# Running the sample's selection and small attention between the tiles of group B's heads, with two heads' columns per projection tile

## The reference

```python
h = _rmsnorm(x, pre_w)
z = h @ w_in                                   # (1024 + 8 rows) x 2048 @ 2048 x 6980
qa, ka, va, ga, qs, ks, vs, gs, qi, ki, wi = _split_cols(z)
...
oa = _diff_attention(qa[..., 0, :], qa[..., 1, :], k_split[..., 0, :], k_split[..., 1, :], va_all, lam, q_pos, k_pos)
oa = _rmsnorm(oa, sub_w) * (1.0 - lam_init)
oa = oa.reshape(b, t, D_A) * jax.nn.silu(ga)   # group A, 8 heads
ob = _dsa_attention(qs, ks_all, vs_all, qi, ki_all, wi, q_pos, k_pos, topk)
ob = ob.reshape(b, t, D_B) * jax.nn.silu(gs)   # group B, 8 query heads on 2 key-value heads
o = jnp.concatenate([oa, ob], axis=-1) @ w_out
x = x + _rmsnorm(o, post_w)
x = x + jax.nn.sigmoid(x @ w_pg + b_pg) * (p @ w_pe)

# inside _dsa_attention, per block of queries
rel = jax.nn.relu(jnp.einsum('bqhd,bsd->bqhs', qqi, ki))
score = jnp.where(vis, jnp.einsum('bqhs,bqh->bqs', rel, ww), -jnp.inf)
_, idx = lax.top_k(score, topk)                # 256 positions per query
kg, vg = k[idx], v[idx]
s = jnp.where(ok, jnp.einsum('bqngd,bqknd->bqngk', qq, kg) * scale, -jnp.inf)
o = jnp.einsum('bqngk,bqknd->bqngd', jax.nn.softmax(s, axis=-1), vg)
```

## Time and profile before

| what | value |
|---|---|
| median of 3 runs | 3878.92 us (3878.88 to 3885.64) |
| profiled execution, its time | 3885.66 us |
| its span in the trace | 3884.0 us, mean granted clock 0.945 |
| PE busy | 3462.2 us, 89% of the span |
| PEld busy | 2731.1 us, 70% |
| DVE busy | 1499.6 us, 39% |
| ACT busy | 845.5 us, 22% |
| POOL busy | 511.6 us, 13% |

### The profile page before, as it was taken

One profiled execution on the slowest core, in us unless ns is written; L12 is line 12 of the kernel. 1 busy time (PEld: TensorE's weight loads), 2 busy tenths in 40 slices (PEclk: granted clock), 3 DMA queues, 4 the chain that ended last, 5 costly groups with the idle time before them and its releaser, 6 DMA issues. The chain is left out here.

```text
span 3884.0 us, 51115 instructions
## 1 busy us (share of the span) xinstructions
PE 3462.2 (89%) x19443; PEld 2731.1 (70%) x19473; DVE 1499.6 (39%) x2854; ACT 845.5 (22%) x1870; POOL 511.6 (13%) x464
## 2 busy tenths in 40 slices
PE   5979999999998988997186899899889999999999
PEld 3667677777776666775133777777768888788887
DVE  2037777777767777622562111111100002311111
ACT  4011344444421212121001122222210002200000
POOL 0002333333332323300003000000000000000000
PEclk9989999999999999998597899999999999999999
DMA  9775677776776756743002011110310111210102
GB/s 343 247 216 147 225 238 255 230 256 222 255 232 216 223 202 219 243 143 104 0 1 65 22 28 39 42 29 6 130 53 24 43 38 62 92 49 24 49 24 87
DMA packets 357958, 497.61 MB, mean 128 GB/s; under 512 B 59793, under 2 KB 280234, under 8 KB 356578
## 3 DMA queue, kind: packets, MB, share of 16 engines
q1 hardware_dynamic: 353440, 486.12, 39.1%
q0 software_dynamic: 1536, 4.20, 0.4%
q10 hardware_dynamic: 2770, 4.46, 0.3%
HBM read 466.81 MB, written 27.90 MB: 127 GB/s over the span
## 5 line engine op out<-in xcount | busy, mean ns | idle before, releaser
L1155 PE MATMUL Z<-W,hT 128*128 128x256 f32 x4608 | 1073.7, 389 | 3.0 <-PEq L116 3.0
L1155 PEld LDWEIGHTS Z<-W,hT 128*128 128x128 f32 x4608 | 869.3, 193 | 210.5 <-issue 97.7
L2079 PE MATMUL Z<-W,hT 128*128 128x256 f32 x2048 | 455.7, 381 | 4.3 <-PE DB L2090 2.3
L2012 PE MATMUL Z<-W,hT 128*128 128x256 f32 x2048 | 446.5, 380 | 1.3 <-ACT small L2141 1.3
L2079 PEld LDWEIGHTS Z<-W,hT 128*128 128x128 f32 x2048 | 390.2, 191 | 61.0 <-issue 7.8
L2012 PEld LDWEIGHTS Z<-W,hT 128*128 128x128 f32 x2048 | 389.2, 191 | 57.2 <-issue 4.6
L781 POOL TENSOR_TENSOR big<-big,qib 128x256 f32<-128x256 f32 x256 | 232.8, 927 | 874.6 <-DMA big<-in_cache_idx_k_dram 718.6
L928 DVE TENSOR_REDUCE page_sc<-big 128x16 f32<-128x1024 f32 x256 | 309.5, 1209 | 1.2 <-POOL big L785 0.6
L917 DVE TENSOR_TENSOR big<-big,qb 128x1024 f32<-128x1024 f32 x192 | 258.5, 1347 | 63.7 <-DMA qb<-zs_d 45.9
L1715 PE MATMUL Z<-W,hT 128*128 128x256 f32 x896 | 210.1, 395 | 0.0
L1715 PE MATMUL DB<-W,hT 128*128 128x256 f32 x896 | 198.8, 380 | 0.0
(11 more groups left out here) (483 smaller groups left out, 3457.0 us busy)
## 6 DMA issues: line engine op xcount, KB each, us to landing
big<-in_cache_diff_k_dram SPq DMA_DIRECT2D x256, 512.0 KB, 4.5
big<-in_cache_diff_v_dram SPq DMA_DIRECT2D x256, 512.0 KB, 5.0
W<-in_w_in_dram SPq DMA_DIRECT2D x27, 2048.0 KB, 10.0
W<-in_w_in_dram SPq DMA_DIRECT2D x72, 512.0 KB, 7.1
W<-in_w_in_dram SPq DMA_DIRECT2D x16, 1024.0 KB, 7.2
W<-in_w_out_dram SPq DMA_DIRECT2D x8, 2048.0 KB, 12.3
W<-in_w_ple_gate_dram SPq DMA_DIRECT2D x8, 2048.0 KB, 8.2
big<-in_cache_idx_k_dram SPq DMA_DIRECT2D x256, 32.0 KB, 4.1
```

The lines of the kernel that those rows point to most:

```text
L1155: mm = pe.matmul(Z[b][:, 0:CW], hT[:, 8 * f + k, n * P:(n + 1) * P], Wr[:, q % 3, k, :], start=(f == 0 and k == 0), stop=(f == 1 and k == 7))
L2012: mm = pe.matmul(Z[t % 2][:, 0:CW], hT[:, k, t * P:(t + 1) * P], W[:, s, k, :], start=(k == 0), stop=(k == KT - 1))
L2079: pe.matmul(Z[b][:, 0:CW], hT[:, k, t * P:(t + 1) * P], W[:, 1 - s, k, :], start=(k == 0), stop=(k == KT - 1))
```

## The change

The tail of group A, the selection and group B's heads become one block. The queries and gates of group B are projected in eight chunks of 256 columns that each hold one kind, queries or gates, of a pair of heads. Their weights come as contiguous 256 columns in halves of 1 MB (`half`, a ring of three), and a tile is projected in two half tiles of 8 matrix products (`project(c, n, f)`). Chunk 0, the first pair's queries, is projected first, with the threshold's counts 0 to 15 between its 16 half tiles. Then 64 tile slots follow, four pairs `s` of 16 slots `x`; slot `k = 16 s + x` is tile `t = k % 8` of head `h = k // 8`. Chunks 1 to 7 are projected in the first 56.

On TensorE a slot is: scores of tile `k`, place 0, first half tile, place 1, transposes of the probabilities, in some slots the output's transposes (`turn`) or new queries (`queries`), place 2, second half tile, place 3, value product. At a place a step of the selection may stand (`decode`). Scores now use `S[0]` alone, the transposes `S[1]`; a projection accumulates in `Z[0]` or `Z[1]`, the value product goes to `TB`, and all decode steps use `DB`. Counts 16 to 32 stand in slots 0 to 8, ranks in 9 and 10, the one-hots of the eight rows in slots 12 to 19 (picks to slot 20), keys and row scores in 23 to 30, the softmax from 31, values in 35 to 42, and the sample's final normalization from 43. The one-hot ring has eight rows, and the picks go to four column groups of the array (`32 * g`), which the copy `picked` takes out. The gathers stand in GpSimd's sequence behind two heads' gate products, four buffers of key or value rows in a ring.

Also: the gate products go from VectorE to GpSimd (`silu`, `output`), except for the last head's; VectorE scales the value product without the gate (`natural`). A pair's rotation is done at once, in slot `x = 8`. Stores of group B's transposed outputs go to SyncE's queue. The last two heads' transposed outputs are copied straight into `hT`, with no store and no read back. The sigmoids stand in slots `x = 0` and `x = 2` of a pair, the last two in slots 56 and 57.

What leaves TensorE's sequence in the selection and in the heads:

```diff
-for n in range(33):
-    pe.wait_ge(b_cnt, n + 1)
-    pe.matmul(TB[:, 0:NB], ones[:, :], cnt, start=True, stop=True).then_inc(b_tot, 1)
...
-for n in range(NPG):
-    u = b * NPG + n
-    pe.wait_ge(b_oh, u + 1)
-    mm = pe.matmul(dst[0:2, 0:TOPK], ids[:, u, :], oneh[:, u % 4, :], start=(n == 0), stop=(n == NPG - 1))
-    mm.then_inc(b_ohu, 1)
-    if n % 2 == 0:
-        k = n // 2
...
-for t in range(NT):
-    pe.wait_ge(h_x, NT * H + t + 1)
-    for f in range(F(t + 1) - F(t)):
-        pe.wait_ge(h_tf, 1 + FB * H + F(t) + f)
-        turned(lambda b: e12[:, t % 2, b * P:(b + 1) * P], f, min(4, t + 1 - 4 * f))
-        if f == 0 and t + 1 < NT:
-            scores(m, u, t + 1)
-    if not last:
-        project(m1, u1, t)
-    pe.wait_ge(h_tf, 1 + FB * H + F(t + 1))
-    pe.wait_ge(h_o, 1 + NT * H + t)
-    for b in range(t + 1):
...
```

TensorE now, chunk 0 and the slots:

```diff
+NPAIR = HB // 2
+NSLOT = 2 * NT
+QCHUNK = {0: 0, 1: 1, 3: 2, 5: 3}
+GCHUNK = {2: 0, 4: 1, 6: 2, 7: 3}
+chunk_at = lambda s, x: 1 + 2 * s + x // NT if s < NPAIR - 1 else (7 if x < NT else None)
+RANK_AT, HOT_AT, K_AT, SOFT_AT, V_AT, END_AT = 9, 12, 23, 31, 35, 43
...
+for i in range(4 * NT // 2):
+    n = 2 * (i // 4) + i % 2
+    project(0, n, i % 4 // 2)
+    total(i)
...
+queries(0)
+queries(1)
+for s in range(NPAIR):
+    for x in range(NSLOT):
+        k, t, h = NSLOT * s + x, x % NT, 2 * s + x // NT
+        c = chunk_at(s, x)
+        scores(k)
+        decode(k, 0)
+        if c is not None:
+            project(c, t, 0)
+        decode(k, 1)
+        pe.wait_ge(h_x, k + 1)
+        if k:
+            pe.wait_ge(h_tc, k)
+        else:
+            pe.wait_ge(h_qc, 2)
+        for b in range(t + 1):
+            mm = pe.transpose(S[1][:, b * P:(b + 1) * P], e12[:, k % 2, b * P:(b + 1) * P], ident[:, :])
+        mm.then_inc(h_t, 1)
+        if s and x in (3, 5):
+            turn(2 * s - 2 + (x == 5))
+        if s < NPAIR - 1 and x in (10, 15):
+            queries(2 * (s + 1) + (x == 15))
+        if s == NPAIR - 1 and x == 11:
+            turn(HB - 2)
+        decode(k, 2)
+        if c is not None:
+            project(c, t, 1)
+        decode(k, 3)
+        pe.wait_ge(h_tc, k + 1)
+        if k:
+            pe.wait_ge(h_nat, k)
+        else:
+            pe.wait_ge(h_qc, 2)
+        for b in range(t + 1):
+            mm = pe.matmul(TB[:, 0:HD], pT[:, b, :], vg[:, h // 4, b, :], start=(b == 0), stop=(b == t))
```

TensorE, the decode steps at the places:

```diff
+def decode(k, place):
+    if k < RANK_AT and place in (1, 3):
+        n = 16 + 2 * k + place // 2
+        if n < 33:
+            total(n)
+    r = k - RANK_AT
+    if r in (0, 1) and place in (1, 3):
+        pe.wait_ge(b_eq, 1 + r)
+        if place == 3:
+            pe.wait_ge(b_prc, r + 1)
+        pe.matmul(DB[:, 0:NB * NS], ones[:, :] if place == 1 else below, eqm, start=True, stop=True).then_inc(b_pre, 1)
+    b = k - HOT_AT
+    if 0 <= b <= NB:
+        if place == 0 and b >= 1:
+            pick(b - 1, 24)
+        if place == 1 and b >= 1:
+            pick_turn(b - 1)
+        if place >= 1 and b < NB:
+            pick(b, 8 * (place - 1))
+    b = k - K_AT
+    if 0 <= b < NB:
+        if place == 1:
+            key_turn(b)
+        if place == 3:
...
```

VectorE, the decode steps of a slot (behind its maximum), the order in a slot, and the one-hots:

```diff
+if k < RANK_AT:
+    bit(15 + 2 * k)
+    if 16 + 2 * k < 32:
+        bit(16 + 2 * k)
...
+if HOT_AT <= k < HOT_AT + NB:
+    for lo in range(0, NPG, 8):
+        one_hot(k - HOT_AT, lo, lo + 8)
...
+for s in range(NPAIR):
+    for x in range(NSLOT):
+        k = NSLOT * s + x
+        if k:
+            natural(k - 1)
+        maximum(k)
+        decode(k)
+        if s < NPAIR - 1 and x == NT:
+            rotate(s + 1)
+        if s == NPAIR - 1 and x == NSLOT - 1:
...
```

```diff
+def one_hot(b, lo, hi):
+    rk3 = three(rkm)
+    for n in range(lo, hi):
+        u = b * NPG + n
+        if u >= 8:
+            dve.wait_ge(b_ohu, u - 7)
+        dve.tensor_scalar(oneh_at(u), iotaj, rk3[:, b, n:n + 1], None, ALU.is_equal).then_inc(b_oh, 1)
```

ScalarE in a slot:

```diff
...
+exps(k)
+if HOT_AT + 1 <= k < HOT_AT + 1 + NB:
+    picked(k - HOT_AT - 1)
+act.wait_ge(h_t, k + 1)
+if k:
+    act.wait_ge(h_pv, k)
+act.activation(pTf[:, 0:(t + 1) * P], S[1][:, 0:(t + 1) * P], ACT.Copy).then_inc(h_tc, 1)
+if s and x in (3, 5):
+    turned(2 * s - 2 + (x == 5))
+if s < NPAIR - 1 and x in (10, 15):
+    queries(2 * (s + 1) + (x == 15))
+if s == NPAIR - 1 and x == 11:
+    turned(HB - 2)
+if K_AT <= k < K_AT + NB:
+    act.wait_ge(b_kt, k - K_AT + 1)
+    act.activation(ktb, DB[:, :], ACT.Copy).then_inc(b_ktc, 1)
+if k == SOFT_AT + 1:
+    act.wait_ge(b_sc, NB + 2)
+    act.activation(ssb[:, 0:257], ssb[:, 0:257], ACT.Exp, scale=SC_B, bias=rmax, accum_out=rsm).then_inc(b_e, 1)
+if k == END_AT + 1:
+    act.wait_ge(b_o, 2)
+    act.activation(sqa, DB[:, 192:256], ACT.Sqrt, scale=1.0 / HD, bias=eps).then_inc(b_qs, 1)
```

GpSimd's gate products and gathers, and SyncE's loads of half chunks:

```diff
+for s in range(NPAIR):
+    if s:
+        for h in (2 * s - 2, 2 * s - 1):
+            silu(h)
+            output(h)
+    if s == 1:
+        pool.wait_ge(b_idx, 1)
+        pool.wait_ge(h_st, 16)
+        for j in range(NB + 4):
+            gather(j)
+    if s == 2:
+        for j in range(NB + 4, 2 * NB):
+            gather(j)
```

```diff
+def half(q):
+    c = q // 2
+    if q >= 3:
+        sp.wait_ge(h_wu, q - 2)
+    lo = QS + 2 * HD * QCHUNK[c] if c in QCHUNK else GS + 2 * HD * GCHUNK[c]
+    sp.dma_start(Wr[:, q % 3, :, :], win[:, 8 * (q % 2):8 * (q % 2) + 8, lo:lo + CW]).then_inc(h_w[q % 3], 16)
```

## The result

The changed kernel takes 3622.18 us (median of 4 runs, 3618.84 to 3625.59), the kernel before 3881.77 us beside it (4 runs, 3878.88 to 3885.64): a ratio of 0.9331, with a 95% interval of 0.9315 to 0.9347.

A forecast was written before the change was run, and what follows sets the result against it. TensorE bounds the heads, while some 330 us of single-step chains hold little matrix work. Terms of 782 us replace 1032, giving 3629 us against the median; 3632 us was said, range 3595 to 3705.

The forecast's parts named there:

- tail of A: From group A's last value product into the new block: only a wait for stores and a barrier left, 5 us.
- chunk 0 with counts 0 to 15: First pair's query projection with threshold counts between half tiles: 3.8 us per step, 65 us in all, bounds 60 and 72.
- change to the slots: Between chunk 0 and the first slot: rotation, two sets of transposes and two copies, uncovered, 7 us, bounds 5 and 10.
- seven heads and decode work: Slots with projections: 571 us for heads at 80.7 each plus slot changes, and 57 us for the selection and attention steps.
- last head: Final slots, without projection and with one score buffer: steps follow one another, 62 us, bounds 42 and 85.
- end: Behind the heads, up to the output projection: last store and reload gone, normalization and last transposes remain, 15 us.
- the cover that the prediction named: In chunk 0, VectorE's 2.6 us per count run under the next half tile, with 0.9 us to spare.
- The held slots: Rival, slots with projections: late VectorE makes TensorE wait at the transposes, heads stay near 90 us, 3695 us; chance 0.14.
- the picks' term: Slots with one-hots: TensorE waits partly for one-hots and the picks cost 2 us, 3.8 per row, 31 in all.
- the rival of the low clock: Last head: serial steps drop TensorE to 1.2 GHz, doubling some 22 us of work, 3654 us; inside the forecast's 0.68.
- The search was not hidden: Rival, counts and picks: all their VectorE time falls on TensorE's path, 112 us more, 3745 us; chance 0.06.
- The slower case: Rival, all slots: waits keep TensorE's clock at 0.50, tiles take 14.2 us instead of 7.1, about 4030 us; chance 0.03.

The follow-up runs named there:

- The run without the cover: Against the changed kernel, every slot's first half tile stands behind the transposes of the probabilities instead of ahead of them; 3786.8 us, ratio 0.9756.
- the filling products: Changed kernel plus unused matrix products in the last head's slots, four ahead of the transposes and two ahead of the value product; 3611.3 us, ratio 0.9296.

## Why the prediction was right, step by step

| term | predicted, us | measured, us | read from |
|---|---|---|---|
| tail of A | 5 | 5.2 | stretch |
| chunk 0 with counts 0 to 15 | 65 | 62.2 | stretch |
| change to the slots | 7 | 7.5 | stretch |
| seven heads and decode work | 571 + 57 | 624.8 | ends of value products |
| last head | 62 | 63.5 | stretch |
| end | 15 | 14.8 | 2568.6 to 2583.4 |
| sum | 782 | 778.0 | |

The sum is 4 us high. Another 3 of the 10 us stand between the 3629 that the sum gives and the 3632 that was said, for which no reason was given. The last 3 are the run: the stages that did not change were 13 us shorter in the trace after, of which 10 drop out against the medians (the profile before lay 6.7 us above its median, the one after 3.3 below).

Where the 253.9 us went, by the same rows: the selection and the small attention had taken 328, and chunk 0 and the decode work take 62.2 and 60.6, which is 205 less; the heads take 564 without the decode work instead of 633, 69 less; tail and end give 9. The last head gives back 21.5, the change to the slots 7.5. What else changed (gate products on GpSimd, stores on SyncE's queue, the last outputs straight into `hT`) was not tried one by one.

**Tail and chunk 0.** Right. One step of chunk 0, as the timeline has it:

```profile
1823.63 0.28 PE L1860 MATMUL DB<-big,ones 128*128 128x8 f32 x2
1823.77 3.70 PE L1801 MATMUL Z<-W,hT 128*128 128x256 f32 x16
1827.30 0.28 PE L1860 MATMUL DB<-big,ones 128*128 128x8 f32 x2
```

The pitch is 3.67 us, where 3.8 were taken (the term is 3 us high), and no row shows idle time: the cover that the prediction named is there. The second half of the weights came in time.

**Seven heads.** The 80.7 us of matrix work per head were measured as 80.7 in head 6, and as 80.0 to 82.0 without the decode work; the 0.1 per slot for one more change of operand did not show. The run without the cover shows that heads and decode work both hang on the half tile ahead of the transposes. The held slots did not come: 1.0 us of waits for exponentials in 56 slots.

**Decode work.** Nearly right in size (57; 60.6), but not in its parts. Counts and ranks were put at 7 and cost 2: 0.8 us is what head 0 lost with its counts, and 1.3 what head 1 has over head 6 with the ranks alone. The picks were put at 31 and cost 35.9. The step said that TensorE would stand idle for the one-hots; the trace has only 1.9 us of idle time there, and the wait shows as long pick rows: eight picks take 0.39 us where their rows are ready and 2.11 where each one waits for VectorE. In slot 16 and slot 17 of the changed kernel:

```profile
2062.16 0.39 PE L1867 MATMUL DB<-page_sc,big 128*2 128x256 bf16 x8
...
2062.88 2.11 PE L1867 MATMUL DB<-page_sc,big 128*2 128x256 bf16 x8
...
2071.51 2.35 POOL L1455 TENSOR_TENSOR seen<-seen,scr 128x1024 f32<-128x1024 f32 x1 [254.42 <-ACT scr L1524]
...
2071.96 4.66 DVE L1668 TENSOR_SCALAR page_sc<-big 128x256 bf16<-128x256 f32 x3
...
2074.03 2.44 POOL L1462 TENSOR_TENSOR seen<-seen,kiT 128x1024 f32<-128x1024 f32 x1 [0.18 <-POOL seen L1455]
```

What the step left out are the transpositions of the picked rows (line 1877, 8 x 0.50 us) and GpSimd's gate products. The prediction has these products only as what stands ahead of the gathers ("behind two heads' gate products") and as a delay of the maximum in the rival of the held slots, and the picks' term has no price for them: while they run, three one-hots take 4.66 us. Moving them away, with the sigmoids, gave 3.2 us. Keys, scores and values were put at 18 and a microsecond for the softmax, and cost 22.7: of the 3.7 us too few, 2.4 are in the list of waits above, where TensorE waits behind each of the eight key transposes (line 1890) for their end. The gathers and the weights are free, as said: no transfer is among TensorE's waits in the heads.

**Last head.** The sum is right, 62 against 63.5, and its working is wrong. It added busy times at the old clock to 59 and half of two sigmoids. Measured are 51.6 us of chain at the full clock, at most, and 12 that the low clock adds in this trace. So the rival of the low clock did come, at 6 to 12 us and not 22, and a chain that was put 10 us too long made room for it; that the two errors cancel is luck. TensorE's waits in the last head, which are those that the prediction named as its sign:

```profile
PE S L2001 <- ACT e L1507: 17.2, 8, 3.3
PE TB L2019 <- ACT pT L1561: 5.2, 7, 1.1
```

The rule cited beside that rival (the Trainium skill, TensorE: Matmul & The Clock Gate, Part 1) agrees with the trace in direction: the clock fell to 0.50 in the short slots, and stayed at 1.00 with the filling products.

**Rivals.** The search was not hidden only in the run that put it in a row, and cost 2.4 us per round and not the 3.23 with which that rival was priced. The slower case was far: the clock in the slots is 1.00. Two sums of the prediction are 1 us high, which changes nothing: 3.8 x 8 is 30, and 3632 + 112 is 3744.

## What to carry to other kernels

A chain of small steps on other engines costs a matrix engine almost nothing if one piece of matrix work of its own, longer than the step, stands between any two links: a round of the search, 2.4 us, went under a half tile of 3.5. Where the step is longer it costs more: the 32 one-hots of a row, 0.27 us each, went through four places of a slot, and the picks cost 36 us. In all 33 rounds, 256 picks and a softmax went under a chunk of projection and seven heads for some 60 us; before, they and that chunk's work had held the core for 330. The last user of such a pattern has no cover left: give it back its second buffer. And price a wait of TensorE twice, once as time and once as the clock that it may cost.

## What was not expected of the hardware

VectorE's one-hots (fp32 in, bf16 out) come to a stop while GpSimd multiplies: three in 4.66 us beside 4.8 us of products, four in 5.33 beside 4.8, against 0.27 us each alone. The third of the three ends 0.15 us behind the second product, and with the products moved away no row is long. The Trainium skill, SBUF — State Buffer, section "SBUF: two separate sides", describes a port pair that the two engines share and that one of them holds for a whole instruction while the other is blocked; these rows agree with it.

Eight picks spread over four column groups of the array take 0.39 us, 49 ns each; in one column group before, two took 0.38.

Table loads between sigmoid and exponential take 1.28 us in the changed kernel as well, and were not what made the last head long: its filled version has the same four loads in 51.6 us, the one with two buffers in 41.2. The two loads ahead of the sigmoids of the last head, and the sigmoids (busy us, mean ns, idle before):

```profile
L1524 ACT ACT_TABLE_LOAD x2 | 2.6, 1283 | 0.0
...
L1524 ACT ACTIVATE scr<-qk 128x1024 f32<-128x1024 f32 x2 | 2.1, 1057 | 0.0
```

ScalarE has no idle time before the load or behind it, so a change of table costs the 1.28 us and no more, and the 5.7 us that the prediction estimated by the other figure did not come. The section with the 1283 ns that it set against that figure (the Trainium skill, ScalarE: Activation LUTs, What ACT_TABLE_LOAD costs) counts a drain besides the load, which the prediction left out; these rows show none.
